# Second self-attention: distance bias and mask added by TensorE in PSUM instead of by VectorE on the way to SBUF

## The reference

```
slopes = 2.0 ** (-8.0 * arange(1, H + 1) / H)           # H = 8 heads
s_own = einsum('bhqd,bhld->bhql', qi, k_own) * Dh ** -0.5
s_own = where(dist_own >= 0, s_own - slopes * dist_own, -inf)
p = softmax(s_own)
out = einsum('bhql,bhld->bhqd', p, v_own)
```

## Time and profile before

| | |
|---|---|
| median of 3 runs | 796.27 us (796.25 to 796.46) |
| profiled execution, its own time | 796.93 us |
| its span, first to last instruction | 795.6 us |
| TensorE busy | 780.2 us, 98% of the span |
| VectorE, ScalarE, GpSimd busy | 575.0, 432.0 and 93.2 us |
| mean granted TensorE clock | 0.999 |

### The profile page before, as it was taken

One profiled execution on the slowest core, in us unless ns is written; L12 is line 12 of the kernel. 1 busy time (PEld: TensorE's weight loads), 2 busy tenths in 40 slices (PEclk: granted clock), 3 DMA queues, 4 the chain that ended last, 5 costly groups with the idle time before them and its releaser, 6 DMA issues.

```text
span 795.6 us, 12288 instructions
## 1 busy us (share of the span) xinstructions
PE 780.2 (98%) x4884; PEld 694.8 (87%) x4884; DVE 575.0 (72%) x782; ACT 432.0 (54%) x644; POOL 93.2 (12%) x145
## 2 busy tenths in 40 slices
PE   6999999999999999999999999999999999999997
PEld 5999999999788888888899998789988988888885
DVE  4986999879886566666667989857556666655664
ACT  5564567563465654545465477557545644444452
POOL 5033970002210000000020000011001100000001
PEclk9999999999999999999999999999999999999999
DMA  9999988984647566566556553455433666666651
GB/s 320 367 286 301 367 271 289 360 289 142 226 119 230 167 213 194 183 190 188 189 181 206 174 153 133 163 178 196 153 106 106 210 191 190 200 187 188 191 178 54
DMA packets 83608, 163.65 MB, mean 206 GB/s; under 512 B 5456, under 2 KB 13840, under 8 KB 83552
## 3 DMA queue, kind: packets, MB, share of 16 engines
q1 hardware_dynamic: 81632, 157.31, 60.0%
q10 hardware_dynamic: 1424, 4.81, 1.9%
q0 software_dynamic: 496, 0.76, 0.5%
HBM read 161.81 MB, written 1.05 MB: 205 GB/s over the span
## 4 chain that ended last, share of the span: by engine, by line
PE 92%; ACT 3%; DVE 2%; issue 1%; DMA 1%; SPq 1%; POOL 1%; DVEq 0%; POOLq 0%; ACTq 0%
PE bank L1810 20%; PE bank L1811 19%; PE bank L1812 19%; PE bank L1875 13%; PE bank L1878 7%; PE bank L1823 2%; PE bank L1829 2%; PE bank L1825 2%; DMA raw_ring<-in_w_in 1%; PE bank L1917 1%; PE bank L2449 1%; PE bank L2068 1%; SPq L464 1%; ACT hi_ring L510 1%; DVE x_residual L1088 1%
## 5 line engine op out<-in xcount | busy, mean ns | idle before, releaser
L962 DVE TENSOR_TENSOR lo_ring<-raw_ring,hi_ring 128x1024 fp32r<-128x1024 f32 x248 | 306.3, 1240 | 152.1 <-ACT hi_ring L510 151.2
L510 ACT CAST hi_ring<-raw_ring 128x1024 fp32r<-128x1024 f32 x248 | 259.4, 1053 | 250.4 <-PE bank L1812 145.5
L1810 PE MATMUL bank<-hi_ring,branch_hi 128*128 128x512 f32 x320 | 126.2, 394 | 0.0
L1810 PE MATMUL bank<-h_hi_lo,hi_ring 128*128 128x256 f32 x432 | 125.7, 291 | 0.0
L1811 PE MATMUL bank<-lo_ring,branch_hi 128*128 128x512 f32 x320 | 124.7, 390 | 0.0
L1812 PE MATMUL bank<-hi_ring,branch_lo 128*128 128x512 f32 x320 | 124.6, 389 | 0.0
L1811 PE MATMUL bank<-h_hi_lo,hi_ring 128*128 128x256 f32 x432 | 122.1, 283 | 0.0
L1812 PE MATMUL bank<-h_hi_lo,lo_ring 128*128 128x256 f32 x432 | 122.1, 283 | 0.0
L1875 PE MATMUL bank<-h_hi_lo,hi_ring 128*128 128x512 f32 x448 | 111.8, 391 | 0.0
L1875 PEld LDWEIGHTS bank<-h_hi_lo,hi_ring 128*128 128x128 f32 x448 | 81.3, 189 | 15.1
L1810 PEld LDWEIGHTS bank<-h_hi_lo,hi_ring 128*128 128x128 f32 x432 | 82.7, 191 | 1.7 <-issue 1.3
(11 more groups left out here) (294 smaller groups left out, 1221.2 us busy)
## 6 DMA issues: line engine op xcount, KB each, us to landing
raw_ring<-in_w_ff SPq DMA_DIRECT2D x128, 512.0 KB, 4.0
raw_ring<-in_w_in SPq DMA_DIRECT2D x64, 512.0 KB, 4.9
raw_ring<-in_w_out SPq DMA_DIRECT2D x16, 512.0 KB, 3.5
raw_ring<-in_w_xkv SPq DMA_DIRECT2D x16, 512.0 KB, 3.7
mem_v<-in_w_ada SPq DMA_DIRECT2D x12, 512.0 KB, 6.8
ada_ring<-in_w_ada SPq DMA_DIRECT2D x10, 512.0 KB, 5.6
mem_k<-in_w_ada SPq DMA_DIRECT2D x10, 512.0 KB, 5.9
raw_ring<-in_w_branch SPq DMA_DIRECT2D x8, 512.0 KB, 5.1
```

The source lines that it names most:

```text
L510: act.copy(m.hi[:, m.slot(u)], m.raw[:, m.slot(u)]).then_inc(s.hi_done, 1)
L962: dve.tensor_tensor(m.lo[:, m.slot(u)], m.raw[:, m.slot(u)], as_f32(m.hi[:, m.slot(u)]), ALU.subtract).then_inc(s.lo_done, 1)
L1810: pe.matmul(out, a_hi, b_hi, start=start, stop=False, skip_group_check=True)
```

## The change

TensorE adds the bias. For each of the 4 parts of a pair `scores` issues one more matmul, which accumulates into the same bank columns: its stationary operand is a 128 by 128 diagonal matrix with 8 times the head's slope, its moving operand `neg_dist`, both fp32r. ScalarE makes the eight diagonal matrices and the rounded copy of `neg_dist` once, after `gain_hi`. VectorE takes only the maxima, two instructions for a pair in place of eight, straight from the banks; ScalarE's exponentials read the banks and write SBUF. The banks are so held until the exponentials are done. To make room in SBUF, the scratch area of GpSimd's software queue is cut to 8192 bytes.

```
+        self.slopes = sb("slope_diagonals", [NH, P], F32R)
+        self.dist_r = sb("neg_dist_rounded", [S], F32R)
...
-    def exponentials(a, g, soft):
+    def exponentials(a, g, soft, b=None):
...
-            ins = act.activation(soft[:, e, c0:c1], soft[:, e, c0:c1], ACT.Exp, bias=negmx[:, i:i + 1], scale=0.125,
+            logits = soft[:, e, c0:c1] if b is None else bank[b + e][:, c0:c1]
+            ins = act.activation(soft[:, e, c0:c1], logits, ACT.Exp, bias=negmx[:, i:i + 1], scale=0.125,
...
     gain_hi(s.in2t, cols[:, G_MIX2:G_MIX2 + KD], m.h_hi)
+    act.wait_ge(s.ident_ok, 1)
+    act.wait_ge(s.dist_ok, 1)
+    for h in range(NH):
+        act.activation(m.slopes[:, h, :], m.ident[:, :], ACT.Copy, scale=8.0 * 2.0 ** (-8.0 * (h + 1) / NH))
+    act.copy(m.dist_r[:, :], m.dist[:, :]).then_inc(s.slopes_ok, 1)
...
-            exponentials(a, g, m.soft2[g])
+            exponentials(a, g, m.soft2[g], pair_bank(g))
...
+    def take_maxima(a, g, b):
+
+        dve.wait_ge(*a.scores.at(g + 1))
+        mx, negmx, _ = m.pair_stats(g)
+        for tt, (c0, c1) in enumerate(CUTS):
+            ins = dve.tensor_reduce(mx.rearrange("p (e t) -> p e t", t=NT)[:, :, tt], m.banks[:, b:b + 2, c0:c1], AX.X,
+                                    ALU.max)
+        ins.then_inc(a.logits.sem, 1)
+        dve.wait_ge(*a.logits.at(g + 1))
+        dve.tensor_scalar(negmx, mx, -0.125, None, ALU.mult).then_inc(a.max.sem, 1)
...
-    dve.wait_ge(s.dist_ok, 1)
...
-            take_scores(a, g, pair_bank(g), pair_bank(g) + 1, m.soft2[g], False)
+            take_maxima(a, g, pair_bank(g))
...
-                           start=tt == 0, stop=not forget, skip_group_check=True)
-        if not forget:
-            scored(a, g, banks, mm)
+                           start=tt == 0, stop=False, skip_group_check=True)
+        if forget:
+            return
+        for e, tt, c0, c1 in parts():
+            mm = pe.matmul(bank[banks[e]][:, c0:c1], m.slopes[:, 2 * g + e, :], m.dist_r[:, P if tt == 0 else 0:],
+                           start=False, stop=True, skip_group_check=True)
+        mm.then_inc(a.scores.sem, 1)
+        free[banks[0]] = free[banks[1]] = a.exp.at(g + 1)
...
         if g == 0:
             pe.wait_ge(s.q2_out, 2)
             pe.wait_ge(s.k2_out, 2)
+            pe.wait_ge(s.slopes_ok, 1)
...
-    nc = bacc.Bacc("TRN2", target_bir_lowering=False, num_devices=1)
+    nc = bacc.Bacc("TRN2", target_bir_lowering=False, num_devices=1, dynamic_dma_scratch_size=8192)
```

More of the change, by code:

```diff
@@ L251, in __init__ @@
             new("pad_zero"))
-        self.ones_ok = new("ones_ok")
+        self.ones_ok, self.slopes_ok = new("ones_ok"), new("slopes_ok")
         self.silu_ok, self.pick_ok, self.rcount_ok = new("silu_ok"), new("pick_ok"), new("rcount_ok")
@@ L1089, in post_add, with take_scores @@
                                      in1=m.x[:, tt, cs], op0=ALU.mult, op1=ALU.add).then_inc(post.x.sem, 1)
-    def take_scores(a, g, b0, b1, soft, forget):
+    def take_scores(a, g, b0, b1, soft):
         dve.wait_ge(*a.scores.at(g + 1))
@@ L1095, in take_scores @@
         for e, tt, c0, c1 in parts():
-            src = bank[b1 if e else b0][:, c0:c1]
             keys = slice(P, S) if tt == 0 else slice(0, S)
[L1098 to L1105, removed]
+            ins = dve.scalar_tensor_tensor(out=soft[:, e, c0:c1], in0=bank[b1 if e else b0][:, c0:c1],
+                                           scalar=m.cum8[:, tt, 2 * g + e:2 * g + e + 1], in1=m.mask[:, keys],
+                                           op0=ALU.add, op1=ALU.add)
         ins.then_inc(a.logits.sem, 1)
@@ L1231, in attention1 @@
             if step == at:
-                take_scores(s.att1, g, 4, 5, m.soft1[g], True)
+                take_scores(s.att1, g, 4, 5, m.soft1[g])
             if step == at + 2:
```

## The result

The changed kernel takes 798.46 us (median of 9, 798.03 to 798.99) against 796.27 us (median of 9, 796.05 to 796.74): 2.19 us more, a ratio of 1.0026, with a 95% interval of 1.0018 to 1.0035. The forecast was 798.1 us. The profiled execution took 798.03 us, the lowest of the nine, with a span of 796.6 us.

A forecast was written before the change was run, and what follows sets the result against it. TensorE was taken to bound the kernel, without idle time in the second self-attention. Its added matmuls cost 1.8 us, all else nothing: span 795.6 to 797.4 us, median 796.27 to 798.1 us; range 797.3 to 799.1 us.

The forecast's parts named there:

- That TensorE sets the time in this stretch, and the rest is cover: Second self-attention, 455 to 545 us: TensorE has no idle time, so each instruction added to it goes straight into the time.
- The sum for TensorE: Second attention's logits: 16 added matmuls at 0.11 to 0.12 us each, 1.8 us; bounds 1.4 and 2.7 us.
- VectorE: Second attention: 32 instructions go and 8 maxima from PSUM come, some 4.6 us less work, worth nothing in time.
- ScalarE's nine instructions: Eight diagonals and one copy behind `gain_hi`: 3.4 us of work, hidden with 2.5 us of cover left.
- The exponentials: Second attention, reading PSUM: at most 0.5 us more ahead of the first normalisation, covered by 1.3 us.
- Banks, waits, scratch area: Longer-held banks have 2.7 us of slack, diagonals are ready over 30 us early, GpSimd's small-load delay is hidden up to 8.6 us.
- A: Rival: added short matmuls nearly free, 1.4 to 1.55 us more, a time near 797.7 us; chance 0.21.
- B: Rival: 0.17 us per added matmul or a stall at a transposition, 2.7 to 3.5 us, near 799.3 us; chance 0.10.
- C: Rival: faster, first loads in the first 100 us land sooner, giving 794.7 us or less; chance 0.06.
- D: Rival: TensorE's order has slack somewhere behind, so the added work costs nothing, 796.3 us; chance 0.03.

The follow-up runs named there:

- five-fold run: Changed kernel with ScalarE making the eight diagonals five times over, same results: 803.35 us, ratio 1.0089 to the kernel before.
- runs with one part alone: Changed kernel with only the 8 added matmuls of 128 columns (797.18 us), or only the 8 of 256 columns (797.34 us), against 796.24 before.
- nine kernels compared: The changed kernel and the eight follow-up kernels, each against the kernel before: ratios from 1.0002 to 1.0089.
- the same merge in the first attention: Kernel before with small scratch area, first attention's sums done by one 384-column matmul per head instead of 128 plus 256: 796.68 us, ratio 1.0005.

## Why the prediction was right

**That TensorE sets the time in this stretch, and the rest is cover.** Shown: with the added matmuls left out the distance is 0.01 us from that of the kernel before.

**The sum for TensorE.** 1.8 us, between 1.76 and 1.92; the distance grew by 1.87. The 0.44 us for four read from the first attention measured 0.47 here, where the four stand in a row and not between matmuls of a unit; whether that makes the difference was not tried. That the load of the stationary operand sets the price of the short ones agrees with 0.106 us each and with the 0.05 to 0.06 us behind loads of 64 columns, and was not tested by itself.

**VectorE.** 4.6 us less was forecast, 4.4 came, worth nothing, as said. The two maxima were put at 0.42 and 0.7 us and take 0.420 and 0.680.

**ScalarE's nine instructions.** Mis-sized but hidden: 3.4 us were worked out from the normalisation's copies, and they took 1.9 us (420.21 to 422.10), so the cover left was 3.9 us where I had 2.5. ScalarE's busy time rose by 0.8 us and not by about 3. The error lay on the safe side and did not touch the forecast. The five-fold run shows that this cover is real and ends. That the work would begin to cost beyond the cover was right; what a stall costs then was put too low in that run's expectation.

**The exponentials.** Taken as dearer from PSUM by up to 0.07 us each, they are cheaper by 0.02 (474 against 495 ns for 256 columns). The row I took, of the attention to the memory, has its scale in a column of SBUF, and this one a constant; the extra may lie there, which was not tried.

**Banks, waits, scratch area.** None showed a cost between the two points, as said. TensorE's busy time rose by 2.5 us and the span by 1.0, where I had said that they would rise alike; the difference is TensorE's idle time, 15.4 us in the profile before and 13.9 here.

**The rivals.** A, short matmuls nearly free: excluded by the runs with one part alone. B, a new wait: TensorE has no idle time from 455 to 547 us in the changed kernel, and a matmul costs 0.117 us, not 0.17. C and D: excluded by the 1.87 us and the ratio.

**What stays open.** The medians differ by more than the distances in all nine kernels compared, by 0.09 to 0.46 us (0.32 in the changed kernel). All nine have the smaller scratch area and so other addresses. Each is inside its own interval, and the run with that area alone has 0.16 us, but all have the same sign, though they share their runs of the kernel before. Whether there is a cost of 0.3 us outside the part that I compared, the runs don't settle. The sum had nothing for it: with the distance alone the median would have been 798.14 us, and the other 0.32 us of the measured 2.19 are not explained by the prediction.

## What to carry to other kernels

Where one engine has no idle time at all, as TensorE here, moving an operation onto it costs its full price, however much it relieves the others; price it from the distance between starts of the same instruction in the same trace, not from its duration. An fp32r matmul with its own 128 by 128 stationary operand cost about as much with 128 moving columns as with 256 here (0.106 and 0.113 us), so parts that share it should be one matmul: 384 columns in one cost 0.17 us where two cost 0.23. A saving is subject to the same test: of the same merge in the first attention only what lay behind TensorE's wait for VectorE showed, 0.1 of 0.5 us.

## What the runs showed of the hardware that I had not expected

- A single stall of 3.2 us of a TensorE that had been busy throughout was followed by some 3.5 us at half the granted clock (matmuls 0.21 us apart from 432.7 to 436.2), 1.6 us of extra time. The clock fell after the work had resumed (matmuls at 431.96 to 432.43 still start 0.12 us apart) and not in the stall. This is one trace: the mean granted clock of the four executions of that kernel was 0.998 (the traced one), 0.994, 0.994 and 0.997, with spans of 801.7, 802.3, 802.9 and 801.5 us.
- ScalarE copies 128 columns with a constant scale at 0.20 us from start to start (8 in 1.6 us), where its normalising copies with a scale from SBUF take 0.37 on average of 128 and 256 columns.
